# The start of the expert lookup on one core: the order of the first gate and norm steps, the placing of the query steps, and the batch sizes

## The chip, the cores and the metric

One core of a Trainium2 chip runs the kernel. Its five engines (TensorE or PE, VectorE or DVE, ScalarE or ACT, GpSimd or POOL, SyncE or SP) each run an instruction stream of their own and are ordered by semaphores alone. The metric is the device time of one execution in microseconds (us); several executions are run and their median is given.

## The reference, cut to what matters

The program computes two transformer blocks for 512 tokens of 1024 features. The last part of the second block, which the change touches, is a lookup of experts: each token picks, for each of 8 heads, the best 16 of 16384 one-neuron experts, and each pick needs that expert's row of `u_tab` and its row of `v_tab`.

```python
q = (xc @ w_pq).reshape(P_CHUNK, P_HEADS, 2, P_DK // 2)
s = jnp.einsum('thpd,hpkd->thpk', q, sub_keys)
s_top, i_top = lax.top_k(s, P_TOPK)                       # 16 of 128, two halves of each head
cand = s_top[..., 0, :, None] + s_top[..., 1, None, :]    # 16 x 16 candidates
best, ci = lax.top_k(cand.reshape(P_CHUNK, P_HEADS, P_TOPK * P_TOPK), P_TOPK)
e1 = jnp.take_along_axis(i_top[..., 0, :], ci // P_TOPK, axis=-1)
e2 = jnp.take_along_axis(i_top[..., 1, :], ci % P_TOPK, axis=-1)
expert = e1 * N_KEYS + e2
gate = jax.nn.softmax(best.astype(jnp.float32), axis=-1).astype(xc.dtype)
act = jax.nn.gelu(jnp.einsum('thkd,td->thk', u_tab[expert], xc), approximate=False)
return jnp.einsum('thk,thkd->td', gate * act, v_tab[expert])
```

`xc` is a normed and modulated copy of the stream x after attention, and the result is added to x before the last norm.

## The kernel before, in words

The 512 tokens are four tiles of 128. All stages up to attention (mixer, gated MLP, convolution, attention) run over all tiles; they are not touched. After them `first_tiles` works on tiles 0 and 1 (`k.late[0]`): output projections (`merge`, `out2_piece`), the second norm (`norm4`), its transposition (`transposed2`: PE turns the tile, DVE and ACT each copy half of it out), and the first four query columns of each tile (`first_queries(i, r)`, eight accumulating matmuls of 128x128 and a copy by ACT for each).

From then on each engine runs its `peer` loop. The picks of a tile are cut into batches of heads, listed in `k.order` (line 2668) as (tile, first head, heads). For tile 0 they are 1, 2, 2 and 3 heads, for each further tile 4 and 4. A head has 16 picks, and a pick is one indirect transfer by POOL (line 2569): 128 rows of 8 KB from the table of experts, u and v side by side, into one of 7 buffers (8 from pick 80, 12 from pick 208). The picks are worked on two at a time, a *group* (`groups`):

- DVE multiplies both rows with the token and adds up (line 2481), ACT takes the gelu (1732), DVE multiplies with the gate (2487), ACT writes two diagonal matrices (1737), PE multiplies them with the v halves into PSUM (1222). When PE has done a pick its buffer is free, and POOL may start the next gather into it (`s.picked`).
- POOL takes the gathers in order. Each batch begins with a wait on `s.expert`, which DVE raises when the batch's expert numbers are written (2420). The fifth gather of all goes to slot 0, a half of weight buffer 2. It waits on the last reader of that buffer, which is `first_queries(1, 3)` on PE.

Beside the groups run two further lists of steps. *Beside steps* (`k.beside`) are the lookup of the next batch, `route(b + 1)`: PE multiplies queries and keys, ACT copies the scores, DVE finds the top 16 in 17 steps; `steps(b)` of them are taken after each group: 3 in batches of one head, 2 of two heads, 1 of more. *Late steps* are the dense work for later: `queries2(0, ...)`, the remaining twelve query columns of tiles 0 and 1 (24 steps of eight matmul instructions; r = 4 to 15), and then `dense(1)`, the same chain for tiles 2 and 3. On PE one late step follows each group. ACT and DVE follow two steps behind (`lagging`). Before the peer loop `first_tiles` takes the first 8 steps of `queries2` at once (`for _ in range(8): next(rest)`), since the scores of the second batch need r = 2 to 5. Weights for the late steps come by SP in units of 2 MB into buffers 0 and 1 as these come free.

In `first_tiles` the orders of the engines around the change are these.

- DVE: `add_out2(1, 1)`, `norm4(1)`, then all of `route(0)`, with `transposed2(1)` after its sixth step.
- ACT: first queries of tile 0, scores of batch 0, `stack(0)` (three copies that lay tile 0 out for two picks at once), `transposed2(1)`, the four copies of `first_queries(1, r)`, the exponential of the first gates (rest of `routing`, line 1684), `stack(1)`, eight query steps.
- PE: scores of batch 0, `transposed2(1)`, `first_queries(1, 0..3)`, eight query steps, and then the groups.

Of the kernel before, what the change touches and what calls it, by code (L numbers as in the profile page):

```python
# [20 lines left out]
NT = SEQ // P  # L21
# [141 lines left out]
class Kernel:  # L163
# [53 lines left out]

    def steps(self, b):
        return 3 if self.picks(b) == TOPK else 2 if self.picks(b) < 3 * TOPK else 1

    def parts(self, b):

# [195 lines left out]
def tensor_program(k):  # L418
# [732 lines left out]
    def first_tiles():  # L1151
# [36 lines left out]
        pe.wait_ge(*ps.of["h2T", 1].free)  # L1188
        for r in range(4):
            first_queries(1, r)  # L1190
        rest = queries2(0, tiles_, 1)
        for _ in range(8):
            next(rest)
        return rest

    def route(b):
        i, h0, nh = k.order[b]
# [9 lines left out]
    def peer(rest):  # L1207
        late = chained(rest, dense(1))
        pick = 0
        for b, (i, h0, nh) in enumerate(k.order):  # L1210
# [4 lines left out]
            for g, (j0, size) in enumerate(k.groups(b)):  # L1215
                for half in range(2):
                    for x in range(size):
                        slot, loads, before = k.gathers[pick + x]
                        if half == 0:
                            pe.wait_ge(s.diag, pick + x + 1)  # L1220
                            pe.wait_ge(s.ld_slot[slot], 16 * loads)
                        last = pe.matmul(acc.pair[k.pick_rows(j0 + x), half, :], k.diags[(pick + x) % DIAGS],  # L1222
                                         k.slots[slot][:, D + half * 512:D + (half + 1) * 512],
                                         start=h0 == 0 and j0 + x < 2, stop=last_batch and j0 + x >= nh * TOPK - 2)
                        if half:
                            last.then_inc(s.picked)
                        elif pick + x == len(k.gathers) - 1:
                            last.then_inc(s.half_picked)
                pick += size
                if g == k.route_begins(b) and b + 1 < len(k.order):  # L1230
                    route(b + 1)
                next(late, None)
            if last_batch:
                ps.held.discard(acc.at)

# [13 lines left out]
def scalar_program(k):  # L1249
# [353 lines left out]
    def transposed2(i):  # L1603
        turn(("h2T", i), k.merged[:, :, i * P:(i + 1) * P], [k.ones[:, 0:1]] * KC)
# [33 lines left out]
    def first_tiles():  # L1638
# [21 lines left out]
        first_queries(0, 3)  # L1660
        stack(0)
        transposed2(1)
        for r in range(4):
            first_queries(1, r)
        for _ in routing:
            pass
        stack(1)
        rest = queries2(0, 4)
        for _ in range(8):
            next(rest)  # L1670
        return rest

    def route(b):
        i, h0, nh = k.order[b]
# [46 lines left out]

    def peer(rest):
        act.wait_ge(s.ident2, 1)
        late = k.lagging(chained(rest, dense(1)))
        pick = group = 0
        for b, (i, h0, nh) in enumerate(k.order):
            beside = k.beside(b, finish_tile, route)
            cf, hid = k.coef[b % 2], k.hidden[b % 2]
            for j0, size in k.groups(b):
# [8 lines left out]
                    pick += 1  # L1738
                for _ in range(k.steps(b)):
                    next(beside, None)  # L1740
                next(late, None)
            for _ in beside:
                pass
        finish_last()
# [14 lines left out]
def vector_program(k):  # L1759
# [558 lines left out]
    def first_tiles():  # L2318
# [14 lines left out]
        add_out2(0, 1)  # L2333
        transposed2(0)
        add_out2(1, 1)
        norm4(1)
        dve.wait_ge(*of["row", 3].free)
        for n, _ in enumerate(route(0)):
            if n == 5:
                transposed2(1)  # L2340
        return k.gap(2 * (2 * PH - 4 - 4))

    def transposed2(i):
        turn(("h2T", i), k.merged[:, :, i * P:(i + 1) * P], [k.ones[:, 0:1]] * KC)
# [26 lines left out]
    def route(b):  # L2371
# [46 lines left out]
        for a, src in enumerate((slice(0, PAIR), slice(PAIR, P))):  # L2418
            for c, dst in enumerate((slice(0, PAIR), slice(PAIR, P))):
                ins = dve.scalar_tensor_tensor(stacked[0][dst, :, :, a], first[src, :, :, c], float(NKEY), second[src, :, :, c], ALU.mult, ALU.add)  # L2420
        ins.then_inc(s.expert)
        dve.wait_ge(s.gate_exp, b + 1)
        dve.tensor_reduce(k.gsum[:, 0, 0:nh], g, AX_X, ALU.add).then_inc(v.up())
        dve.wait_ge(*v.now())
# [40 lines left out]
    def peer(rest):  # L2465
        late = k.lagging(chained(rest, dense(1)))
        pick = group = 0
        for b, (i, h0, nh) in enumerate(k.order):
# [5 lines left out]
            for j0, size in k.groups(b):  # L2474
# [12 lines left out]
                dve.tensor_tensor(cf[:, cut], cf[:, cut], g[:, cut], ALU.mult).then_inc(s.coef)  # L2487
                for _ in range(k.steps(b)):
                    next(beside, None)
                next(late, None)  # L2490
            for _ in beside:
                pass
        finish_last()
# [146 lines left out]
def program(nc, A, out):  # L2640
    with ExitStack() as stack:
# [15 lines left out]
        k.heads_order = [(h + a, i) for h in range(0, AH, 2) for i in range(NT) for a in range(2)]  # L2657
        k.feature_sq = [k.sg[1], k.sg[2], k.sg[1], k.sg[0]]
        k.feature_root = [k.sg[0], k.sg[2], k.sg[1]]
        k.order = [(0, 0, 1), (0, 1, 2), (0, 3, 2), (0, 5, 3)] + [(i, h0, 4) for i in range(1, NT) for h0 in (0, 4)]  # L2660
        count = [0] * 12
        k.gathers = []
        busy, free = {}, deque((2, 3, 4, 5, 0, 1, 6))
# [148 lines left out]
```

## Time and profile before

| | us |
|---|---|
| median of 3 runs | 2815.76 |
| lowest, highest | 2812.87, 2822.55 |
| the profiled execution | 2814.78 |
| its span in the trace | 2813.5 |

| engine | busy us | share of the span |
|---|---|---|
| PE (matmul) | 2291.8 | 81% |
| DVE | 1732.4 | 62% |
| POOL | 741.9 | 26% |
| ACT | 638.4 | 23% |

The span is the time from the first to the last instruction in the trace; 1.3 us of the profiled execution lie around it. The shares are averages over two different halves: to about 1430 us PE is busy nearly always, and from about 1450 us the DMA engines are. In the chain of work that ended last PE has 36% of the span and DMA 31%. All rows below come from the one profiled execution.

### The profile page before, as it was taken

The page shows a single profiled execution, that of the slowest core. Times are in us where ns is not written, and L with a number is a line of the kernel's source. Part 1 is how long each engine was busy: PE and PEld are TensorE (multiplying, and loading weights), DVE is VectorE, ACT ScalarE, POOL GpSimd, SP SyncE. Part 2 cuts the span into 40 slices and gives each one's busy share as a digit, 9 for nine tenths or more (in the row PEclk, how much of TensorE's full clock was granted, in tenths as well). Part 3 has the DMA queues.
Part 4 walks back from the last instruction along what each step waited for, and adds up shares of the span by engine and source line. Part 5 has one row for each costly group of instructions (what it writes and reads, how often), then busy time and mean ns, then how long its engine had stood idle before and what let it go on. Part 6 is the DMA issues. An engine that isn't in the chain of part 4 may idle for free.

```text
span 2813.5 us, 24680 instructions
## 1 busy us (share of the span) xinstructions
PE 2291.8 (81%) x8398; PEld 1294.5 (46%) x8398; DVE 1732.4 (62%) x3796; ACT 638.4 (23%) x1611; POOL 741.9 (26%) x582
## 2 busy tenths in 40 slices
PE   8998999999999999999997777678555656566655
PEld 5756478886444445666664433344222222222222
DVE  2132369985127995666447677767675767667555
ACT  2222220001020003566232111322112211121112
POOL 0000032430000002000014444434444444444442
PEclk9999999999999999999999999899888778787778
DMA  4111124443222121001359999999999999999997
GB/s 164 60 46 45 53 90 179 151 170 147 87 98 85 63 82 68 1 1 60 119 212 371 421 415 421 407 421 419 420 420 420 420 420 419 420 420 420 420 420 297
DMA packets 87307, 687.13 MB, mean 244 GB/s; under 512 B 9848, under 2 KB 10616, under 8 KB 12816
## 3 DMA queue, kind: packets, MB, share of 16 engines
q0 software_dynamic: 73728, 536.90, 46.2%
q1 hardware_dynamic: 12016, 144.09, 13.3%
q10 hardware_dynamic: 1440, 4.57, 0.4%
q8 instruction: 69, 1.13, 0.2%
q14 instruction: 54, 0.44, 0.0%
HBM read 683.42 MB, written 2.10 MB: 244 GB/s over the span
## 4 chain that ended last, share of the span: by engine, by line
PE 36%; DMA 31%; DVE 7%; ACT 3%; POOL 2%; issue 1%; ACTq 0%; DVEq 0%
PE psum L430 20%; DMA slot<-in_experts,expert 19%; DMA weights<-in_experts,expert 11%; PE psum L1222 5%; PE psum L1024 3%; DVE slot L2481 2%; PE psum L1046 2%; PE psum L1032 1%; DVE weights L2481 1%; PE psum L1095 1%; PE psum L1085 1%; POOL xn L2569 1%; PE psum L1117 1%; ACT spare_row L1737 1%; POOL weights L2569 1%
## 5 line engine op out<-in xcount | busy, mean ns | idle before, releaser
L1222 PE MATMUL psum<-slot,spare_row 128*64 128x512 f32 x844 | 387.2, 751 | 112.5 <-ACT spare_row L1737 112.5
L1222 PE MATMUL psum<-weights,spare_row 128*64 128x512 f32 x832 | 305.6, 782 | 190.6 <-ACT spare_row L1737 187.0
L2569 POOL DMA_INDIRECT slot<-in_experts,expert x211 | 251.4, 1192 | 544.4 <-DVE expert L2420 314.1
L1222 PE MATMUL psum<-xn,spare_row 128*64 128x512 f32 x372 | 223.7, 733 | 160.0 <-ACT spare_row L1737 159.0
L2569 POOL DMA_INDIRECT weights<-in_experts,expert x208 | 241.8, 1162 | 279.5 <-PE psum L1222 245.0
L1732 ACT ACTIVATE coef<-hidden 128x2 f32<-128x2 f32 (+1 forms) x257 | 52.3, 203 | 1003.4 <-DVE hidden L2481 1003.4
L1222 PEld LDWEIGHTS psum<-weights,spare_row 128*64 128x64 f32 x832 | 114.4, 164 | 358.5 <-ACT spare_row L1737 295.2
L2481 DVE CUSTOM_DVE_ANT_0 slot<-slot,h_late 128x1024 f32<-128x1024 f32 x147 | 180.0, 1225 | 126.2 <-DMA slot<-in_experts,expert 124.9
L430 PE MATMUL psum<-xnT,weights 128*128 128x264 f32 (+1 forms) x1040 | 245.2, 390 | 1.5 <-ACT mixedT L1399 0.9
L430 PE MATMUL psum<-hT,weights 128*128 128x512 f32 x560 | 243.0, 596 | 1.9 <-ACT hT L1266 1.9
L430 PEld LDWEIGHTS psum<-xnT,weights 128*128 128x128 f32 x1040 | 199.4, 194 | 37.7 <-issue 5.1
L1222 PEld LDWEIGHTS psum<-slot,spare_row 128*64 128x64 f32 x844 | 112.4, 159 | 213.1 <-ACT spare_row L1737 157.9
L2481 DVE CUSTOM_DVE_ANT_0 weights<-weights,h_late 128x1024 f32<-128x1024 f32 x104 | 127.5, 1226 | 96.5 <-DMA weights<-in_experts,expert 95.9
L2119 DVE SCALAR_TENSOR_TENSOR merged<-padded,cols,merged 128x512 f32<-128x512 f32 x240 | 175.2, 749 | 6.4
L1222 PEld LDWEIGHTS psum<-xn,spare_row 128*64 128x64 f32 x372 | 49.9, 156 | 275.4 <-ACT spare_row L1737 242.5
L430 PEld LDWEIGHTS psum<-hT,weights 128*128 128x128 f32 x560 | 106.7, 191 | 137.0 <-issue 134.9
L2523 POOL TENSOR_TENSOR up_sums<-weights 128x1024 f32<-128x1024 f32 x11 | 27.5, 2502 | 522.9 <-DMA weights<-in_w_up 489.8
L1737 ACT ACTIVATE spare_row<-ident,coef 128x64 f32<-128x64 f32 x512 | 150.3, 340 | 59.5 <-DVE coef L2487 59.5
L2569 POOL DMA_INDIRECT xn<-in_experts,expert x93 | 104.1, 1120 | 217.5 <-PE psum L1222 214.6
L2481 DVE CUSTOM_DVE_ANT_0 weights<-weights,hT 128x1024 f32<-128x1024 f32 x104 | 126.9, 1220 | 42.8 <-DMA weights<-in_experts,expert 42.4
L430 PE MATMUL psum<-weights,gT 128*128 128x512 f32 x352 | 152.1, 593 | 0.0
L2481 DVE CUSTOM_DVE_ANT_0 xn<-xn,hT 128x1024 f32<-128x1024 f32 x88 | 107.5, 1221 | 44.0 <-DMA xn<-in_experts,expert 43.8
(401 smaller groups left out, 3489.0 us busy)
## 6 DMA issues: line engine op xcount, KB each, us to landing
weights<-in_w_mod SPq DMA_DIRECT2D x12, 2048.0 KB, 8.5
weights<-in_w_up SPq DMA_DIRECT2D x11, 2048.0 KB, 7.5
weights<-in_w_in SPq DMA_DIRECT2D x8, 2048.0 KB, 8.4
weights<-in_w_pq SPq DMA_DIRECT2D x8, 2048.0 KB, 10.3
weights<-in_w_out SPq DMA_DIRECT2D x6, 2048.0 KB, 9.2
weights<-in_w_in_t SPq DMA_DIRECT2D x4, 2048.0 KB, 7.7
weights<-in_w_down SPq DMA_DIRECT2D x4, 2048.0 KB, 12.4
weights<-in_w_o_mla SPq DMA_DIRECT2D x4, 2048.0 KB, 10.0
```

The costliest lines, as they stand in the source:

```text
L430: last = pe.matmul(out, lhsT, rhs, start=start and n == 0, stop=stop and n == len(pairs) - 1)
L1024: last = pe.matmul(u.pair[:, a, 0:KH], Q[0:QK, h % 4, i * P:(i + 1) * P], K[0:QK, h % 2, a * KH:(a + 1) * KH], start=True, stop=True)
L1032: last = pe.transpose(u.pair[:, j // 3, (j % 3) * P:(j % 3 + 1) * P], L[:, j * P:(j + 1) * P], ident[:])
L1046: last = pe.matmul(u.pair[rows, 0, 0:2 * P], k.values[j][:, (2 * p + a) * VD:(2 * p + a + 1) * VD], k.probsT[q][:, j, a * 2 * P:(a + 1) * ...
L1085: last = pe.matmul(u.pair[:, 0, 0:len(tiles_) * P], w[:, c, v * P:(v + 1) * P], k.heads[:, cut, c, :], start=c == 0, stop=c == KC - 1)
L1095: last = pe.matmul(u.pair[:, 0, :], k.merged[:, c, i * P:(i + 1) * P], w[:, c, :], start=c == 0, stop=c == KC - 1)
L1222: last = pe.matmul(acc.pair[k.pick_rows(j0 + x), half, :], k.diags[(pick + x) % DIAGS], k.slots[slot][:, D + half * 512:D + (half + 1) * 512],
L1732: act.activation(cf[:, j0:j0 + size], hid[:, j0:j0 + size], ACT.Gelu).then_inc(s.gelu)
L1737: act.activation(k.diags[pick % DIAGS], k.ident2[:], ACT.Copy, scale=cf[:, j:j + 1]).then_inc(s.diag)
L2119: ins = dve.scalar_tensor_tensor(acc, src, col(k, "dw_w", j * KC + n), acc, ALU.mult, ALU.add)
L2481: ins = dve.tensor_tensor_reduce(slot[:, 0:D], slot[:, 0:D], rows_of[j % 2], 1.0, 0.0, ALU.mult, ALU.add, hid[:, j:j + 1])
L2569: pool.indirect_dma_start(k.slots[slot], None, k.A["experts"], bass.IndirectOffsetOnAxis(ap=k.expert[b % 2][:, j:j + 1], axis=0))\
```

## The change

It does five things. On DVE `norm4(1)` moves behind the first 18 steps of `route(0)`, that is, behind the expert numbers of the first batch (a new `yield` after `then_inc(s.expert)` makes the place), and `transposed2(1)` moves behind the end of `route(0)`. On ACT the exponential of the first gates moves ahead of the copies of `first_queries(1, r)`, and `stack(1)` moves behind the query steps (`later_tiles`). The eight query steps ahead of the peer loop go on every engine. In the first two batches two late steps follow each group instead of one (`late_steps`). The batches of tile 0 are 1, 1, 2 and 4 heads instead of 1, 2, 2 and 3.

```diff
--- before.py
+++ after.py
@@ -218,6 +218,9 @@
     def steps(self, b):
         return 3 if self.picks(b) == TOPK else 2 if self.picks(b) < 3 * TOPK else 1
 
+    def late_steps(self, b):
+        return 2 if b < 2 else 1
+
     def parts(self, b):
 
         h0, nh = self.order[b][1:]
@@ -1188,10 +1191,7 @@
         pe.wait_ge(*ps.of["h2T", 1].free)
         for r in range(4):
             first_queries(1, r)
-        rest = queries2(0, tiles_, 1)
-        for _ in range(8):
-            next(rest)
-        return rest
+        return queries2(0, tiles_, 1)
 
     def route(b):
         i, h0, nh = k.order[b]
@@ -1229,7 +1229,8 @@
                 pick += size
                 if g == k.route_begins(b) and b + 1 < len(k.order):
                     route(b + 1)
-                next(late, None)
+                for _ in range(k.late_steps(b)):
+                    next(late, None)
             if last_batch:
                 ps.held.discard(acc.at)
 
@@ -1660,15 +1661,16 @@
         first_queries(0, 3)
         stack(0)
         transposed2(1)
+        for _ in routing:
+            pass
         for r in range(4):
             first_queries(1, r)
-        for _ in routing:
-            pass
+        return queries2(0, 4)
+
+    def later_tiles(rest):
+        yield from rest
         stack(1)
-        rest = queries2(0, 4)
-        for _ in range(8):
-            next(rest)
-        return rest
+        yield from dense(1)
 
     def route(b):
         i, h0, nh = k.order[b]
@@ -1721,7 +1723,7 @@
 
     def peer(rest):
         act.wait_ge(s.ident2, 1)
-        late = k.lagging(chained(rest, dense(1)))
+        late = k.lagging(later_tiles(rest))
         pick = group = 0
         for b, (i, h0, nh) in enumerate(k.order):
             beside = k.beside(b, finish_tile, route)
@@ -1738,7 +1740,8 @@
                     pick += 1
                 for _ in range(k.steps(b)):
                     next(beside, None)
-                next(late, None)
+                for _ in range(k.late_steps(b)):
+                    next(late, None)
             for _ in beside:
                 pass
         finish_last()
@@ -2333,12 +2336,15 @@
         add_out2(0, 1)
         transposed2(0)
         add_out2(1, 1)
+        routing = route(0)
+        for _ in range(18):
+            next(routing)
         norm4(1)
+        for _ in routing:
+            pass
         dve.wait_ge(*of["row", 3].free)
-        for n, _ in enumerate(route(0)):
-            if n == 5:
-                transposed2(1)
-        return k.gap(2 * (2 * PH - 4 - 4))
+        transposed2(1)
+        return k.gap(2 * (2 * PH - 4))
 
     def transposed2(i):
         turn(("h2T", i), k.merged[:, :, i * P:(i + 1) * P], [k.ones[:, 0:1]] * KC)
@@ -2419,6 +2425,7 @@
             for c, dst in enumerate((slice(0, PAIR), slice(PAIR, P))):
                 ins = dve.scalar_tensor_tensor(stacked[0][dst, :, :, a], first[src, :, :, c], float(NKEY), second[src, :, :, c], ALU.mult, ALU.add)
         ins.then_inc(s.expert)
+        yield
         dve.wait_ge(s.gate_exp, b + 1)
         dve.tensor_reduce(k.gsum[:, 0, 0:nh], g, AX_X, ALU.add).then_inc(v.up())
         dve.wait_ge(*v.now())
@@ -2487,7 +2494,8 @@
                 dve.tensor_tensor(cf[:, cut], cf[:, cut], g[:, cut], ALU.mult).then_inc(s.coef)
                 for _ in range(k.steps(b)):
                     next(beside, None)
-                next(late, None)
+                for _ in range(k.late_steps(b)):
+                    next(late, None)
             for _ in beside:
                 pass
         finish_last()
@@ -2657,7 +2665,7 @@
         k.heads_order = [(h + a, i) for h in range(0, AH, 2) for i in range(NT) for a in range(2)]
         k.feature_sq = [k.sg[1], k.sg[2], k.sg[1], k.sg[0]]
         k.feature_root = [k.sg[0], k.sg[2], k.sg[1]]
-        k.order = [(0, 0, 1), (0, 1, 2), (0, 3, 2), (0, 5, 3)] + [(i, h0, 4) for i in range(1, NT) for h0 in (0, 4)]
+        k.order = [(0, 0, 1), (0, 1, 1), (0, 2, 2), (0, 4, 4)] + [(i, h0, 4) for i in range(1, NT) for h0 in (0, 4)]
         count = [0] * 12
         k.gathers = []
         busy, free = {}, deque((2, 3, 4, 5, 0, 1, 6))
```

## Rows read from the trace of the kernel before

**Rows 1.** Page, span in 40 equal slices: GB/s that the DMA engines moved.

```profile
GB/s 164 60 46 45 53 90 179 151 170 147 87 98 85 63 82 68 1 1 60 119 212 371 421 415 421 407 421 419 420 420 420 420 420 419 420 420 420 420 420 297
```

**Rows 2.** Page, DMA queue: packets, MB, share.

```profile
q0 software_dynamic: 73728, 536.90, 46.2%
```

**Rows 3.** Windows: PE, PEld, DVE, ACT, POOL busy; PEclk, DMA share, GB/s.

```profile
1442.00:1448.00 6.00, 4.99 (x23) 5.00 (x24) 4.29 (x18) 1.23 (x5) 1.04 (x1) 0.50 0.00 0
1448.00:1452.00 4.00, 4.00 (x38) 4.00 (x37) 0.00 (x0) 0.55 (x2) 2.91 (x4) 1.00 0.84 274
1472.00:1482.00 10.00, 9.53 (x43) 5.80 (x43) 8.36 (x38) 1.53 (x5) 4.32 (x6) 1.00 0.97 346
1482.00:1494.00 12.00, 8.82 (x35) 4.94 (x34) 11.07 (x31) 2.05 (x8) 5.52 (x4) 1.00 1.01 418
1494.00:1504.70 10.70, 8.19 (x32) 4.74 (x32) 9.92 (x28) 4.44 (x9) 1.51 (x2) 1.00 0.42 158
1448.00:1516.00 68.00, 53.96 (x252) 36.90 (x250) 40.84 (x123) 19.63 (x47) 24.95 (x23) 1.00 0.88 346
1600.00:1650.00 50.00, 38.63 (x151) 21.87 (x148) 39.21 (x128) 9.63 (x29) 19.84 (x17) 0.93 1.01 418
```

**Rows 4.** Timeline, first lookup: start, us, engine, line, operation.

```profile
1433.23 0.16 DVE L1765 RECIPROCAL stat<-stat 128x1 f32<-128x1 f32 x1 [1.54 <-ACT stat L1259]
1434.69 0.39 ACT L1273 ACTIVATE scores<-psum 128x256 f32<-128x256 f32 x1 [0.58 <-PE psum L1204]
1435.89 0.48 DVE L2348 MAX8 top<-scores 128x8 f32<-128x128 f32 x2
1438.70 1.13 DVE L1777 TENSOR_SCALAR merged<-psum,ones 128x128 f32<-128x128 f32 x4
1439.75 0.42 DVE L2386 TENSOR_TENSOR scores<-top 128x256 f32<-128x256 f32 x1
1445.98 0.69 DVE L2420 SCALAR_TENSOR_TENSOR expert<-picked 64x8 uint32<-64x8 f32 x4
```

**Rows 5.** Timeline, POOL: first, fifth, eighth and seventeenth gather.

```profile
1446.96 1.12 POOL L2569 DMA_INDIRECT slot<-in_experts,expert  x1 [304.68 <-DVE expert L2420]
...
1453.05 0.94 POOL L2569 DMA_INDIRECT weights<-in_experts,expert  x1 [1.23 <-PE psum L430]
...
1471.60 0.94 POOL L2569 DMA_INDIRECT slot<-in_experts,expert  x1 [15.12 <-PE psum L1222]
...
1502.88 0.94 POOL L2569 DMA_INDIRECT slot<-in_experts,expert  x1 [9.47 <-DVE expert L2420]
```

**Rows 6.** Timeline, second tile's transposes, query matmuls, and the first gates.

```profile
1438.07 1.04 PE L441 MATMUL psum<-ident,hT 128*128 128x128 f32 x8
...
1441.81 1.14 ACT L1266 ACTIVATE merged<-psum,ones 128x128 f32<-128x128 f32 x4
...
1443.01 9.77 PE L430 MATMUL psum<-merged,weights 128*128 128x128 f32 x64 [3.90 <-ACT merged L1266]
...
1454.40 0.22 ACT L1684 ACTIVATE gate_exp<-gate_exp 128x16 f32<-128x16 f32 x1
...
1454.65 0.17 DVE L2423 TENSOR_REDUCE gsum<-gate_exp 128x1 f32<-128x16 f32 x1 [7.97 <-ACT gate_exp L1684]
...
1455.05 0.69 DVE L2430 TENSOR_TENSOR gate<-gate_exp,gsum 64x8 f32<-64x8 f32 x4
```

**Rows 7.** Timeline, the block ahead of the first group, and the first groups.

```profile
1452.61 13.98 PE L1117 MATMUL psum<-merged,weights 128*128 128x256 f32 x64
...
1467.03 1.28 ACT L1732 ACT_TABLE_LOAD   x1
...
1469.43 2.03 PE L1222 MATMUL psum<-slot,spare_row 128*64 128x512 f32 x8 [2.84 <-ACT spare_row L1737]
...
1472.38 1.89 PE L1117 MATMUL psum<-merged,weights 128*128 128x256 f32 x8
1474.20 1.94 PE L1222 MATMUL psum<-slot,spare_row 128*64 128x512 f32 x8
```


## The prediction

> **What bounds the kernel now.** I read the page's slices first. To about 1430 us the DMA engines are far from full; from 1548 us on they move 407 to 421 GB/s in every slice but the last [rows 1]. The software queue alone carries 536.90 MB [rows 2], which is 512 gathers of 1.049 MB (128 rows of 8 KB). So the second half of the span is a stream of gathers at about 420 GB/s, 2.5 us each, and engine work beside it costs nothing unless it starves the stream. The span can change in two ways only: the stream starts earlier or later, or it has fewer or more holes. That is read from the windows at its start, then from the timelines of the engines that feed it.
>
> Between 1442 and 1448 nothing moves [rows 3]. The first gather is issued at 1446.96 [rows 5], and between 1448 and 1452 the DMA share is 0.84 [rows 3]: moving begins 0.16 x 4 = 0.64 us after 1448, some 1.7 us after the issue. From 1448 to 1516 the mean is 346 GB/s, 23.5 MB [rows 3]. At 420 it would be 28.6 MB; the missing 5.0 MB are 12.0 us. About half of that is one hole: between 1494 and 1504.7 the share is 0.42 [rows 3], 6.2 us idle, because the seventeenth gather (first of the second batch) waited for its expert numbers until 1502.88, with POOL idle for 9.47 us [rows 5]. The rest is a low rate: 346 GB/s from 1472 to 1482, against 418 from 1482 to 1494 [rows 3]. The tail after the last gather is untouched. So 12.0 us of holes and a later or earlier start are all that is at stake, 0.4% of the time.
>
> **The change part by part.**
>
> *Norm behind the first expert numbers.* DVE's lookup began at 1435.89, behind the norm, though its scores were there at 1434.69 + 0.39 = 1435.08: 0.8 us. `transposed2(1)` inside the lookup took from 1438.70 to 1439.75: 1.05 us [rows 4]. Without both, the numbers that were done at 1445.98 + 0.69 = 1446.67 are done at 1444.8, and the first gather is issued at 1445.1 rather than 1446.96, 1.85 us earlier. Taken alone this is the gain that the edit aims at.
>
> *What the norm delays.* The norm took from 1433.23 to the end of its last operation just after 1435.89, 2.75 us with the overlap [rows 4]; it now ends at 1447.6. Then a chain follows that lay under other work before:
> - PE's eight transposes, 1.04 us at the full clock [rows 6], up to twice that at half: PE's work before them ends as the transposes of before begin, about 1438.1, so it has been idle for over 9 us. I take 1449.2.
> - ACT's `transposed2(1)`, 1.14 us [rows 6]: 1450.4.
> - the exponential: a table load of 1.28 [rows 7] and 0.22 [rows 6]: 1451.9. (Before, it was done at 1454.62.)
> - DVE's gates, which are ahead of its `transposed2(1)` in the new order: from 1454.65 to 1455.74, 1.1 us [rows 6]: 1453.0. Behind this wait on DVE are queued `transposed2(1)` and the first products.
> - DVE's `transposed2(1)`, 1.13 us [rows 4]: 1454.2.
> - PE's `first_queries(1, 0..3)`, 64 instructions: 9.77 us [rows 6], half of it at the low clock: the granted clock was 0.50 from 1442 to 1448 [rows 3]. They begin at 1454.3 rather than 1443.01 and end at 1464.1 rather than 1452.78.
>
> The last line is the important one. The fifth gather waits for exactly this end: it was issued at 1453.05, and POOL had sat idle 1.23 us for PE's query matmuls [rows 5]. POOL is in order, so the sixth and seventh are queued behind it. After the change the fifth goes out at 1464.1 + 0.27 = 1464.4. Four gathers, 4.19 MB, move from 1446.8 and at 346 to 420 GB/s are done between 1456.8 and 1458.9; then the DMA engines have nothing (SP's next weights wait on PE too) until 1464.4 + 1.7 = 1466.1. So the hole at 1494 is exchanged for one of 7 to 9 us at 1458, and the 1.85 us are worth nothing, since the same four gathers are done before 1464 either way.
>
> *The query block taken out.* The block of 64 instructions held PE from 1452.61 for 13.98 us [rows 7]. Without it PE and ACT reach the first group straight after the queries: last copy at about 1464.4, and from there as before from 1467.03 (table load) to 1469.43 (first matmul), 2.4 us [rows 7]: the first group at 1466.8 instead of 1469.43, the eighth gather at 1469.0 instead of 1471.60 [rows 5].
>
> *Two steps after each group.* PE's group becomes 1.94 us of picks and two steps of 1.82 to 1.89 [rows 7], 5.6 us. DMA needs 2 x 2.5 = 5.0 us a group, and eight steps, which are four groups, release a weight unit of 2 MB, 5.0 us more: 25.0 us of DMA work for 22.4 us of PE. In the mean DMA stays the slower one. ACT takes a query copy a group behind PE, so it waits for a step that ended before PE began the group.
>
> *Batches 1, 1, 2, 4.* The second batch's lookup has one head, like the first's, 1446.67 - 1435.89 - 1.05 = 9.7 us of DVE [rows 4], spread over groups 1 to 6 (three steps each). Group 5's matmuls begin at 1466.8 + 0.6 + 5 x 5.6 = 1495.4 (0.6 for the scores' matmuls, an estimate from a step's 1.89 for eight instructions). From there ACT's copy 0.4, table 1.3, gelu and gate 0.4 lead to group 6's gate at 1497.5, and the last sixth of the lookup, 1.6, to the numbers at 1499.1: the seventeenth gather at 1499.4, moving at 1501.1, against 1502.88 before. By then DMA has had, from 1466.1, twelve gathers and the fourth query unit (now released by step 8, about 1490): 12 x 2.5 + 5.0 = 35.0 us, to 1501.1. The hole just closes. The third batch's two heads are looked up beside one head's groups, as the second batch's were before, but with another weight unit in the queue. The fourth batch's four heads are looked up at two steps a group where three were: the nearest rows are the window 1600 to 1650, DVE busy 39.2 of 50 us with the DMA share at 1.01 [rows 3]. One head more adds a third to three heads' lookup; by 9.7 us a head that is at most 9.7 on about 52 us for nine groups, so DVE's 41 become 51. It just fits. I take 0, with 0 and 5 us as ends.
>
> *`stack(1)` later.* Three copies, off the path before; they now meet the second batch's exponential in one group of ACT. 0, at most 1 us.
>
> *Sum.* By 1516 the kernel before has moved 23.5 MB. After, 4.19 MB by 1466, and then 49.9 us at a rate that I take between its two neighbours, 346 for 10 us and 418 for 12 [rows 3], 385 GB/s: 19.2 MB, 23.4 in all. 0.1 MB short is 0.3 us at 420. At 418 throughout it is 25.0 MB, 3.7 us gained; at 346, 21.5 MB, 4.9 lost. Query matmuls without a low clock would be 2.3 us shorter. The profiled execution took 2814.8, 1.0 below the median of the runs; with 0.3 more it is 2815.1. I say 2815.
>
> **The rivals.**
> 1. *The restart isn't held.* If the fifth gather went out at its old place behind the fourth, the hole at 1458 is not there, and of 12.0 us only the ramp is left, about 1: 2804. For it: this is what the edits would give with the fifth buffer free. Against it: the row of the fifth gather names PE's query matmuls as what released it, and nothing in the diff frees that buffer sooner. The same number would come if the norm's chain were much shorter than I work out.
> 2. *PE stays cold: slower.* PE is idle twice, from 1438.1 to 1447.6 and from 1449 to 1454, where there was one gap of 3.9 us, after which the clock was 0.50, the 1.2 GHz level, for 6 us [rows 3, 6]. If it stays there through the queries and the first group, the 64 instructions take about 15 us instead of 9.77 (+5.1), and the first group 11.2 instead of 5.6 (+5.6): 10.7 us more hole, 2825. It decides from the second group at the low clock on. Against it: in the trace the clock was back at 1.00 in the window from 1448, 5 us after work began, and PE then has work without a break. The Trainium skill, TensorE: Matmul & The Clock Gate, Part 1, says that the throttled state is the default and that only sustained activity releases it. By that rule the two gaps speak against this change; the trace agrees on the fall and on the return.
> 3. *PE becomes the feed's limit.* If weight units don't fill the gaps, 16 groups lose 0.6 us each, 9.6 us, less up to 5 us that a unit hides: 2820 to 2825. For it: 5.6 is more than 5.0. Against it: seven buffers hold 17.5 us of transfers.
>
> **How the numbers follow.** A difference of 0.3%, 8.4 us, is about what a measurement of this kernel can tell. Forecast 0.68 (2815, its own range 2809 to 2822, within 0.3%). Rival 1 0.10 (faster). Rival 2 0.13 (slower). Rival 3 0.09, two thirds of it within 0.3% of the median of before. So faster 0.10, same 0.74, slower 0.16. The range 2807 to 2825 leaves out rival 1 and the upper part of rival 2.
>
> **What would show it.** Right: first gather 1.9 us earlier, fifth some 11 us later behind PE's L430, an empty DMA window from 1458 to 1466, no POOL wait for expert numbers of more than a few us before the seventeenth, DMA at 1.0 from 1505 on. Wrong: a fifth gather before 1460; clock 0.50 beyond 1461; DMA shares below 0.95 between 1510 and 1640, which would put the loss into the two steps a group or the four heads.

## The result, and the profile after

| | before | after |
|---|---|---|
| median of 20 runs each | 2818.47 us | 2827.15 us |
| lowest, highest | 2808.37, 2829.31 | 2816.97, 2837.17 |
| ratio after / before, 95% interval | | 1.0024 (1.0013 to 1.0036) |
| the profiled execution, its span | 2814.78, 2813.5 | 2825.49, 2824.2 |

The change costs 0.24%, 6.8 us. That is within the 0.3% that the forecast gave as the likeliest, but the time lies 2 us above the stated range. The two spans are 10.7 us apart, and not all of that is the change: the copy of the first scores, ahead of which nothing is altered, comes at 1437.95 after and came at 1434.69 before [rows 4]. From that copy to the end it is 1386.2 us against 1378.8: 7.4 us in these two executions, close to the 6.8 of the medians' ratio.

To see where they went I count *lost transfer time*: from 5 us after the first scores' copy to 1300 us after it, the span is cut into stretches, and each stretch loses its length times (420 - GB/s) / 420, by the windows. If transfers are what limits this part, the difference of the sums must be near the 7.4 us, and it is: 30.2 - 23.2 = 7.0.

| us after the first scores' copy | before | after |
|---|---|---|
| 5 to 22, start of the stream | 10.4 | 7.9 |
| 22 to 32 | -0.1 | 9.1 |
| 32 to 60 | 2.8 | 3.0 |
| 60 to 81, ahead of the second batch | 7.3 | 0.1 |
| *up to 81* | *20.4* | *20.1* |
| 100 to 140, ahead of the third batch | 0.0 | 3.7 |
| 140 to 240, beside the fourth batch's lookup | 0.7 | 5.0 |
| 240 to 450 | 2.0 | 1.5 |
| sum | 23.2 | 30.2 |

The windows behind it, of the kernel after (first two: 4 us each, from 12 and from 20 us after the copy; then 22 to 32, 60 to 81, 100 to 140, 140 to 240), in the columns of [rows 3]:

```profile
1450.00:1454.00 4.00, 1.97 (x8) 1.57 (x8) 0.97 (x1) 0.96 (x4) 3.39 (x3) 0.50 0.91 328
1458.00:1462.00 4.00, 3.96 (x18) 3.96 (x19) 2.28 (x4) 0.14 (x1) 0.00 (x0) 0.50 0.71 299
1459.95:1469.95 10.00, 8.20 (x57) 8.01 (x56) 0.33 (x2) 2.57 (x6) 1.22 (x2) 0.81 0.09 36
1497.95:1518.95 21.00, 20.09 (x89) 13.05 (x89) 11.43 (x29) 5.08 (x14) 7.59 (x8) 1.00 1.00 417
1537.95:1577.95 40.00, 35.17 (x157) 23.14 (x157) 28.45 (x74) 12.17 (x29) 12.54 (x12) 1.00 0.94 381
1577.95:1677.95 100.00, 74.08 (x249) 33.72 (x245) 78.78 (x224) 17.84 (x58) 41.88 (x34) 0.93 0.98 399
```

The same three last stretches of the kernel before:

```profile
1494.69:1515.69 21.00, 14.07 (x56) 7.96 (x56) 14.80 (x34) 5.82 (x15) 8.98 (x7) 1.00 0.69 273
1534.69:1574.69 40.00, 28.73 (x114) 16.46 (x112) 29.46 (x77) 9.13 (x27) 16.39 (x14) 0.95 1.01 420
1574.69:1674.69 100.00, 76.47 (x276) 39.85 (x272) 73.57 (x200) 17.23 (x58) 42.41 (x35) 0.92 1.01 417
```

The hole ahead of the second batch (273 GB/s before) is closed (417), but between 22 and 32 us almost nothing moves (36 GB/s, share 0.09); and the two later stretches, full before at 420 and 417, run at 381 and 399.

The timeline of the kernel after, from the first scores to the eighth gather, which answers to [rows 4 to 7]:

```profile
1437.95 0.38 ACT L1274 ACTIVATE scores<-psum 128x256 f32<-128x256 f32 x1 [0.58 <-PE psum L1204]
1438.37 0.49 DVE L2354 MAX8 top<-scores 128x8 f32<-128x128 f32 x2 [3.42 <-ACT scores L1274]
...
1447.48 0.69 DVE L2426 SCALAR_TENSOR_TENSOR expert<-picked 64x8 uint32<-64x8 f32 x4
1448.46 1.12 POOL L2577 DMA_INDIRECT slot<-in_experts,expert  x1 [302.91 <-DVE expert L2426]
...
1449.75 1.23 DVE L2292 TENSOR_TENSOR hT<-hT,ctxn 128x1024 f32<-128x1024 f32 x1
1451.03 1.97 PE L444 MATMUL psum<-ident,hT 128*128 128x128 f32 x8 [9.54 <-DVE hT L2292]
...
1453.04 1.15 ACT L1267 ACTIVATE merged<-psum,ones 128x128 f32<-128x128 f32 x4 [7.99 <-PE psum L444]
...
1455.49 0.22 ACT L1686 ACTIVATE gate_exp<-gate_exp 128x16 f32<-128x16 f32 x1
...
1456.14 0.69 DVE L2437 TENSOR_TENSOR gate<-gate_exp,gsum 64x8 f32<-64x8 f32 x4
1456.87 1.12 DVE L1780 TENSOR_SCALAR merged<-psum,ones 128x128 f32<-128x128 f32 x4
1458.05 10.11 PE L433 MATMUL psum<-merged,weights 128*128 128x128 f32 x64 [5.05 <-DVE merged L1780]
...
1468.42 0.94 POOL L2577 DMA_INDIRECT weights<-in_experts,expert  x1 [14.16 <-PE psum L433]
...
1470.88 3.50 PE L1222 MATMUL psum<-slot,spare_row 128*64 128x512 f32 x8 [2.73 <-ACT spare_row L1739]
1474.59 0.94 POOL L2577 DMA_INDIRECT slot<-in_experts,expert  x1 [2.39 <-PE psum L1222]
```

After the lookup come first gather, norm, transposes, ACT's half, exponential, gates, DVE's half, queries, fifth gather and first group, in the order that the prediction works out. The brackets name the step ahead as what ended the wait at the transposes (norm), ACT's half (transposes), the queries (DVE's half) and the fifth gather (queries). The fifth gather is issued 30.5 us after the scores' copy; before it was 18.4 us [rows 4, 5].

Two waits of POOL for expert numbers remain, and the second one is what the third batch costs (columns as in the timelines above; POOL, DVE, ACT, DVE, POOL):

```profile
1504.92 0.93 POOL L2577 DMA_INDIRECT slot<-in_experts,expert  x1 [6.83 <-DVE expert L2426]
...
1554.53 1.22 DVE L2488 CUSTOM_DVE_ANT_0 slot<-slot,h_late 128x1024 f32<-128x1024 f32 x1 [1.65 <-DMA slot<-in_experts,expert]
...
1555.80 0.20 ACT L1734 ACTIVATE coef<-hidden 128x2 f32<-128x2 f32 x1 [1.06 <-DVE hidden L2488]
...
1558.28 0.72 DVE L2426 SCALAR_TENSOR_TENSOR expert<-picked 64x16 uint32<-64x16 f32 x4
...
1559.26 0.93 POOL L2577 DMA_INDIRECT weights<-in_experts,expert  x1 [12.01 <-DVE expert L2426]
```

The first (6.83 us) costs nothing, since the queue still holds gathers. In the second POOL sits idle 12.01 us. The last products of the group ahead of the numbers themselves waited for a gather (1.65 us, at 1554.53); gelu, gate and the last lookup steps follow, and the numbers are there at 1559.0. By then the stream has run dry:

```profile
1558.00:1560.00 2.00, 2.00 (x10) 1.15 (x7) 1.86 (x8) 0.00 (x0) 0.74 (x1) 1.00 0.20 82
```

Beside the fourth batch's lookup DVE is the slow one. In this window of the kernel after (columns of [rows 3]) it is busy 21.68 of 23 us while the stream falls to 337 GB/s:

```profile
1603.00:1626.00 23.00, 16.11 (x66) 8.89 (x64) 21.68 (x61) 5.98 (x15) 10.12 (x8) 0.99 0.91 337
```

The first products of one group and of the fourth group after it, in the timeline, are 25.5 us apart: 6.4 us a group, where a group's two gathers take 5.0.

```profile
1602.44 1.21 DVE L2488 CUSTOM_DVE_ANT_0 slot<-slot,hT 128x1024 f32<-128x1024 f32 x1
...
1627.98 1.22 DVE L2488 CUSTOM_DVE_ANT_0 slot<-slot,hT 128x1024 f32<-128x1024 f32 x1
```

### The profile page after: what moved, and what is told of

Same layout as the page of the kernel before. It is cut to its first block, busy times and chain, and to the rows that moved or that the text cites. A ratio compares the mean times of both kernels' runs of the same rounds, so it can differ in the third digit from the quotient of the medians.

```text
span 2824.2 us, 24682 instructions
## 1 busy us (share of the span) xinstructions
PE 2299.0 (81%) x8398; PEld 1294.6 (46%) x8398; DVE 1731.4 (61%) x3796; ACT 639.0 (23%) x1611; POOL 739.3 (26%) x582
## 4 chain that ended last, share of the span: by engine, by line
PE 34%; DMA 31%; DVE 7%; ACT 3%; POOL 2%; issue 2%; ACTq 0%; DVEq 0%; POOLq 0%
PE psum L433 19%; DMA slot<-in_experts,expert 16%; DMA weights<-in_experts,expert 15%; PE psum L1222 5%; PE psum L1027 3%; DVE slot L2488 2%; PE psum L1049 2%; PE psum L1035 1%; DVE weights L2488 1%; PE psum L1098 1%; PE psum L1088 1%; POOL weights L2577 1%; PE psum L1120 1%; ACT spare_row L1739 1%; POOL slot L2577 1%
## 5 line engine op out<-in xcount | busy, mean ns | idle before, releaser
L1222 PE MATMUL psum<-slot,spare_row 128*64 128x512 f32 x844 | 397.1, 762 | 100.3 <-ACT spare_row L1739 100.3
L1222 PE MATMUL psum<-xn,spare_row 128*64 128x512 f32 x372 | 239.5, 779 | 165.2 <-ACT spare_row L1739 163.5
## 6 DMA issues: line engine op xcount, KB each, us to landing
weights<-in_w_down SPq DMA_DIRECT2D x4, 2048.0 KB, 12.2
```

## Experiments

All ten kernels, beside the two. "Span" is the time from the first scores' copy to the end, less that of before; the sum is that of the lost transfer time, less 23.2.

| kernel | 5 to 22 | 22 to 32 | 32 to 60 | 60 to 81 | 100 to 140 | 140 to 240 | sum | span | ratio to before (95%) |
|---|---|---|---|---|---|---|---|---|---|
| after | 7.9 | 9.1 | 3.0 | 0.1 | 3.7 | 5.0 | +7.0 | +7.4 | 1.0024 (1.0013 to 1.0036) |
| norm_only | 7.9 | 9.1 | 8.5 | 5.5 | 0.1 | -0.2 | +13.1 | +13.4 | 1.0046 (1.0023 to 1.007) |
| norm_back | 9.8 | -0.1 | 4.0 | 1.4 | 2.4 | 4.5 | -0.7 | -0.7 | 0.9998 (0.9981 to 1.0015) |
| slot6_fifth | 7.8 | 6.7 | 5.3 | 0.1 | 4.6 | 4.3 | +7.5 | +7.7 | 1.0029 (1.0009 to 1.0049) |
| heads_1133 | 8.0 | 9.0 | 2.7 | 0.6 | 7.2 | 0.0 | +4.2 | +5.7 | 1.0024 (0.9998 to 1.005) |
| stack_back | 8.1 | 8.5 | 5.9 | 1.4 | 1.9 | 5.5 | +8.5 | +9.0 | one run |
| unit_off | 8.0 | 8.6 | 0.5 | 0.3 | 7.7 | 5.0 | +8.6 | +3.8 | one run |
| steps4 | 7.9 | 9.1 | 2.5 | -0.1 | 0.0 | 5.2 | +2.3 | +1.9 | 1.0000 (0.9978 to 1.0022) |
| spread | 8.0 | 9.0 | 2.3 | 0.0 | -0.2 | 1.4 | -1.2 | -1.6 | 0.9977 (0.9964 to 0.9989) |
| four_ahead | 9.8 | -0.1 | 1.1 | 1.9 | 0.0 | 0.0 | -7.9 | -7.5 | 0.9975 (0.9955 to 0.9995) |
| four_ahead_s4 | 10.3 | -0.2 | 1.6 | -0.1 | 0.0 | 0.0 | -7.5 | -8.4 | 0.9983 (0.9964 to 1.0001) |

81 to 100 (norm_only 3.5, all others within 0.1) and 240 to 450 us (0.0 to 4.0) are in the sums. Each kernel's stretches come from one profiled execution. Sum and span agree within 1 us but for two kernels: unit_off moves 2 MB (4.8 us) less, and in heads_1133 1.5 us stay unexplained.

### The norm's part: norm_only and norm_back

To the kernel before, on DVE (and on ACT the rest of `routing` ahead of `first_queries(1, r)`):

```diff
-        norm4(1)
-        dve.wait_ge(*of["row", 3].free)
-        for n, _ in enumerate(route(0)):
-            if n == 5:
-                transposed2(1)
+        routing = route(0)
+        for _ in range(18):
+            next(routing)
+        norm4(1)
+        for _ in routing:
+            pass
+        dve.wait_ge(*of["row", 3].free)
+        transposed2(1)
```

> The kernel before with only the first part of the change: norm, second tile's transposes and the first gates' exponential in the new order; the block of eight query steps, one step a group and batches 1, 2, 2, 3 as before. Theory: the fifth gather goes out about 30 us after the first scores' copy, with the same empty stretch of some 9 us; the block of 14 us then holds the first group until about 46 us after the scores, 11 us later than before, so that a second empty stretch of some 6 us follows when the seven gathers are done; in all 10 to 14 us over before, 0.4 to 0.5%. Rival (the early expert numbers pay for the wait): 2 us under to 3 us over before.

Two of its windows, 22 to 32 and 32 to 60 us after its scores' copy at 1443.89:

```profile
1465.89:1475.89 10.00, 10.00 (x67) 9.77 (x67) 0.32 (x2) 2.65 (x6) 1.32 (x2) 0.82 0.09 39
1475.89:1503.89 28.00, 24.69 (x108) 17.13 (x107) 10.37 (x44) 7.42 (x17) 5.89 (x7) 0.94 0.79 292
```

Share 0.09, then 292 GB/s, and 13.4 us in the span: the theory's 10 to 14. So the edit that was to bring the first gather forward costs 13 us by itself, with the query block still ahead of the groups. norm_back takes the same edit out of the kernel after:

> The changed kernel with the order of the norm, the second tile's transposes and the first gates' exponential put back as before; query steps between the groups and batches 1, 1, 2, 4 stay. I count lost transfer time from the copy of the first scores on: (420 - GB/s) / 420 times the length of each window. The changed kernel lost 30.5 us in all, 18.0 of it by 81 us after that copy, where the kernel before lost 23.3 and 20.5. Theory (the hole comes from the fifth gather waiting for the second tile's queries, which the norm's chain delays): fifth gather about 18 us after the scores' copy instead of 30, no empty stretch from 22 to 32 us, the first group some 10 us earlier than in either kernel; lost by 81 us about 12, so 6 us less than the changed kernel, and a time about that of before or just under it. The later losses (3.8 us at the third batch, 4.9 us at the fourth batch's lookup) stay. Rival (two query steps a group limit the feed, and the hole only delays what PE could not take anyway): lost by 81 us stays at 17 to 18 and the time at that of the changed kernel, 0.24% over before.

The 18.0 us that this expectation gives for the kernel after up to 81 us are 20.1 in the table, so its "6 us less" is 14 by the table, and the rival's unchanged value is 20. Its fifth gather and its first group (scores' copy at 1439.63):

```profile
1458.10 0.94 POOL L2574 DMA_INDIRECT weights<-in_experts,expert  x1 [1.36 <-PE psum L433]
...
1465.68 3.77 PE L1222 MATMUL psum<-slot,spare_row 128*64 128x512 f32 x8 [7.85 <-ACT spare_row L1739]
```

The fifth gather is out 18.5 us after the scores' copy, the hole is gone, the first group comes at 26.1 us instead of 32.9, and lost time up to 81 us falls from 20.1 to 15.1, 5.0 less (the first group was expected some 10 us earlier and came 7 earlier, and it took 3.77 us for 2.03 [rows 7]). The time can't be told from that of before. The theory holds, and the rival, by which that loss would not change, falls.

### Which of the two waits behind the norm: slot6_fifth

```diff
-        busy, free = {}, deque((2, 3, 4, 5, 0, 1, 6))
+        busy, free = {}, deque((2, 3, 4, 5, 6, 0, 1))
```

> The changed kernel with one edit: the buffers are given out in the order 2, 3, 4, 5, 6, 0, 1 instead of 2, 3, 4, 5, 0, 1, 6, so the fifth gather goes to a buffer that is free, and the sixth is the first that waits for the second tile's queries. Theory (the stretch of 9.1 us without transfers is the wait on that buffer): five gathers move before the restart, the empty stretch falls by one gather, 2.5 us, to 6.6, and the time by 0 to 2.5 us. Rival (the restart is set by the first group, not by the buffer): the fifth gather goes out early, but the bytes moved by 81 us after the first scores are the same within 0.3 MB.

22 to 32 and 32 to 60 us after its scores' copy at 1444.51:

```profile
1466.51:1476.51 10.00, 8.15 (x57) 7.96 (x56) 0.32 (x2) 2.60 (x6) 1.28 (x2) 0.82 0.33 138
1476.51:1504.51 28.00, 27.12 (x114) 16.42 (x115) 19.91 (x60) 7.62 (x24) 11.13 (x10) 0.94 0.94 341
```

The first window gains 2.4 us (138 GB/s), the second loses 2.3 (341): up to 81 us 19.9 against 20.1, less than 0.1 MB apart. The rival is right here. The buffer makes the visible wait, but the same chain holds the first group as well, and a gather brought forward without a group brought forward moves nothing.

### The later losses: heads_1133, steps4 and spread

```diff
-k.order = [(0, 0, 1), (0, 1, 1), (0, 2, 2), (0, 4, 4)]
+k.order = [(0, 0, 1), (0, 1, 1), (0, 2, 3), (0, 5, 3)]
```

> The changed kernel with batches of 1, 1, 3, 3 heads instead of 1, 1, 2, 4. Theory (each later loss is a lookup that is too large for the groups that it lies beside): the loss at the fourth batch's lookup, 4.9 us at 165 to 200 us after the first scores, falls to under 1 us, as three heads at one step a group leave DVE time; the hole at the third batch's expert numbers grows from 3.8 us to 6 to 8, since three heads are looked up beside eight groups. In all within 2 us of the changed kernel. Rival (both losses come from the two late steps a group and the weights that they call up earlier): both stay where they are, 3.8 and 4.9 us.

100 to 140 and 140 to 240 us after its scores' copy at 1444.04:

```profile
1544.04:1584.04 40.00, 33.53 (x145) 22.27 (x144) 32.71 (x83) 11.25 (x26) 11.74 (x12) 1.00 0.85 344
1584.04:1684.04 100.00, 74.39 (x243) 34.49 (x241) 71.11 (x191) 17.78 (x59) 39.60 (x37) 0.91 1.01 420
```

3.7 becomes 7.2, and 5.0 becomes 0.0, as the theory has it: each loss goes with the size of one lookup. steps4 instead takes the kernel after and gives the lookups beside one-head batches four steps a group instead of three:

```diff
-        return 3 if self.picks(b) == TOPK else 2 if self.picks(b) < 3 * TOPK else 1
+        return 4 if self.picks(b) == TOPK else 2 if self.picks(b) < 3 * TOPK else 1
```

> The changed kernel with four lookup steps instead of three after each group of the batches of one head. The third batch's expert numbers then come one group earlier in the second batch. Theory (the hole at the third batch is the place of the numbers behind the seventh group): loss from 100 to 140 us from 3.8 to under 1.5; the 4.9 us at the fourth batch stay; 2 to 4 us under the changed kernel. Rival (DVE is the limit there, and more steps a group make each group longer by as much): 3 to 5 us lost as before, or earlier in the batch.

The same two stretches of it, scores' copy at 1428.80:

```profile
1528.80:1568.80 40.00, 38.39 (x172) 24.11 (x170) 29.95 (x78) 12.32 (x28) 15.94 (x14) 1.00 1.01 420
1568.80:1668.80 100.00, 76.44 (x243) 33.91 (x244) 78.35 (x232) 18.00 (x59) 42.63 (x35) 0.88 0.99 398
```

420 GB/s: with the numbers one group earlier the hole at the third batch is gone, and the 5.2 us beside the fourth batch's lookup are left. The span is 5.5 us under the kernel after, more than the expected 2 to 4. spread adds to steps4 a slower lookup beside the third batch, two steps and one in turn (after group n, where the call in the loop over groups becomes `steps_after`):

```diff
+    def steps_after(self, b, n):
+        return 2 - n % 2 if b == 2 else self.steps(b)
...
-            for _ in range(k.steps(b)):
+            for _ in range(k.steps_after(b, n)):
```

> The changed kernel with four lookup steps a group in the batches of one head (which lost 25.4 us, 5.2 of it from 140 to 240 us after the first scores), and in the third batch two and one steps in turn instead of two after each group, so that the fourth batch's four heads are looked up over 12 groups instead of 9. Theory (DVE is the limit in those nine groups): the loss from 140 to 240 us falls from 5.2 to under 2, 22 to 23 us lost in all. Rival (the loss there comes from the low clock of PE or from the order of the steps, not from DVE's work per group): it stays at 4 to 6, or the numbers come too late for the 65th gather and open a new hole of 3 us or more at its end.

140 to 240 us after its scores' copy at 1440.76:

```profile
1580.76:1680.76 100.00, 76.87 (x248) 34.99 (x248) 81.31 (x242) 18.01 (x59) 45.24 (x36) 0.93 1.01 414
```

5.2 falls to 1.4 with DVE busier than before (81.3 of 100 us against 78.4). So it was not DVE's work as such, but that nine groups had to carry it. The time is under that of before by 6.5 us over seven runs (3 to 10), the span of the profiled execution by only 1.6; how much of the 6.5 is a first half that came early by chance stays open.

### One execution each: stack_back and unit_off

> The changed kernel with ACT's stack(1), three copies of 1.05 us, back ahead of the groups. In the changed kernel it lies in the same group of the second batch as the exponential and two table loads, 6 us of ACT in a row that end 1.1 us before the next gelu. Theory (the hole at the third batch, 3.8 us, comes from the lookup being queued on DVE behind the products of the seventh group, not from ACT): the hole stays at 3 to 5 us. Rival (the moved copies delay the gelu and so the expert numbers): it falls by 2 to 3 us.

```diff
             first_queries(1, r)
+        stack(1)
         return queries2(0, 4)
```

(and its call in `later_tiles` taken out.) Its stretch from 100 to 140 us:

```profile
1540.42:1580.42 40.00, 38.67 (x171) 24.81 (x168) 31.93 (x84) 9.28 (x27) 15.14 (x14) 0.97 0.98 400
```

The loss there fell to 1.9, between the two expectations; but the copies now hold the first group, 35.1 us after the scores' copy instead of 32.9, and 32 to 81 us lost 4.2 more. A start that differs changes what the queue holds at the third batch, so the run doesn't separate the two.

> The changed kernel with one weight unit not loaded (64 KB of 2 MB of the second w_o_mla unit of tiles 2 and 3, so that their output is worked out from what lay in the buffer): the one that SP issues 106 us after the first scores, beside the last gathers of the second batch. Prediction's view (the unit fills the queue while the third batch's numbers are worked out): without it the loss from 100 to 140 us grows from 3.8 to about 8 us, and the span loses nothing. Rival (the unit delays the gathers that the lookup itself waits for, so it hides nothing): the loss stays at about 4 us, the numbers come some 4 us earlier, and the span falls by the unit's 5 us.

```diff
-                weights(name, unit)
+                weights(name, unit, P if (tiles_, name, unit) == (k.late[1], "w_o_mla", 1) else UNIT)
```

100 to 140 us after its scores' copy at 1442.07:

```profile
1542.07:1582.07 40.00, 37.14 (x168) 23.64 (x164) 29.31 (x78) 12.05 (x27) 14.04 (x14) 1.00 0.84 339
```

7.7 us lost instead of 3.7, 4.0 more, what the prediction's view has. The gather that waits for the numbers also went out 3.3 us earlier (118.0 us after the scores' copy against 121.3), and the span is 3.6 us shorter where 4.8 us of transfers are gone. But not all of that is the edit's: up to 81 us, ahead of the unit, this execution had already lost 2.6 us less (17.5 against 20.1), with the same program. Its first group took 2.03 us where that of the kernel after took 3.50, behind an idle time of the same length:

```profile
1474.06 2.03 PE L1222 MATMUL psum<-slot,spare_row 128*64 128x512 f32 x8 [2.73 <-ACT spare_row L1739]
```

At the last gather of the second batch (107.17 us after the copy against 108.24) 1.1 us of that lead were left, so about 2.2 of the 3.3 us can be the unit's, and of the 3.6 us in the span about 1.0. The unit mainly fills the queue; that it also delays the gathers that the lookup waits for is likely, by some 2 us, but one execution with another start doesn't show it alone.

### Four query steps ahead of the groups: four_ahead and four_ahead_s4

To the kernel before, in the norm's old order and with batches 1, 2, 2, 3, and with two of the late query steps a group in the first batch and one in the others (the loops of PE and of ACT; left out here are `late_steps`, which gives 2 for the first batch and 1 for the others, and DVE's count of the steps that it skips):

```diff
-        for _ in range(8):
+        for _ in range(4):
             next(rest)
...
-                next(late, None)
+                for _ in range(k.late_steps(b)):
+                    next(late, None)
```

> The kernel before with one edit: four query steps instead of eight ahead of the groups (the second batch's scores need no more) and two steps a group in the first batch; order of the norm and batches 1, 2, 2, 3 as before. Theory (the first group, not the first gather, sets what the stream loses in its first 81 us): first group about 27 us after the first scores instead of 35, the hole of 7.3 us ahead of the second batch falls to 1 to 3, in all 17 to 19 us lost instead of 23.3, 0.15 to 0.2% under before. Rival (two steps a group slow the first batch by what the earlier start gains): 22 to 24 us lost, time as before.

60 to 81 us after its scores' copy at 1448.11:

```profile
1508.11:1529.11 21.00, 16.85 (x66) 9.97 (x65) 10.82 (x27) 2.54 (x10) 7.96 (x8) 0.92 0.94 381
```

7.3 us become 1.9, 15.3 are lost in all (expected: 17 to 19), and the time is 0.25% under before (0.05 to 0.45). Half of the query block was not needed before the second batch's scores, and it had held the first group, which comes 26.9 us after the scores' copy instead of 34.7. With four lookup steps a group beside the first batch (the steps4 edit on this kernel):

> The kernel with four query steps ahead (order of the norm and batches 1, 2, 2, 3 as before the change), and four lookup steps instead of three after each group of the first batch. It lost 15.3 us with three, of which 1.9 between 60 and 81 us after the first scores, ahead of the second batch's numbers. Theory (numbers one group earlier close that hole): 1.9 falls to under 0.6, the rest stays, 13 to 15 us lost in all, 0.2 to 0.35% under before. Rival (DVE is full in the first batch, so four steps make each group longer): 15 to 17 us lost, time as with three steps.

```profile
1502.32:1523.32 21.00, 18.31 (x84) 12.14 (x84) 9.59 (x19) 3.31 (x12) 8.43 (x8) 1.00 1.01 421
```

The last hole is closed (421 GB/s from 60 to 81 us), as the theory has it, but 15.7 us are lost in all, in the rival's range, since 240 to 450 us lost 4.0 instead of 2.5 in these executions. The time can't be told from that of four_ahead, nor, by its interval, from that of before.

## Why the prediction was wrong

**The first 81 us: right.** The sum was 0.3 us worse than before; the lost time is 0.3 better, 20.1 against 20.4. The steps hold one by one, measured from the scores' copy: first gather at 10.5 us against 12.3 before, 1.8 earlier (worked out: 1.85); fifth at 30.5 against 18.4, 12 later (11 to 12); an empty stretch of 9.1 us (7 to 9); the seventeenth gather waits for its numbers without a hole (worked out: just closes). POOL's 6.83 us ahead of it are more than the "few us" among the signs, and cost nothing. That the two sums meet within 0.6 us is in part luck: unit_off, the same program up to there, lost 2.6 us less. Rival 1 is out: the fifth gather waited 14.16 us for PE's query matmuls. Its price was too high as well, since norm_back, which has no such wait, still loses 15.1 us up to 81 us.

**The cold clock: a small part of rival 2.** The granted clock was 0.50, the 1.2 GHz level, at 1450 to 1454 and at 1458 to 1462, after PE had been idle 9.54 and then 5.05 us. During the queries it rose to 1.00, and behind the 2.73 us without work ahead of the first group it fell again:

```profile
1464.00:1466.00 2.00, 2.00 (x21) 2.00 (x20) 0.00 (x0) 0.28 (x1) 0.00 (x0) 1.00 0.00 0
...
1472.00:1474.00 2.00, 2.00 (x7) 0.47 (x3) 0.70 (x3) 0.79 (x3) 0.19 (x1) 0.51 0.98 385
```

The queries took 10.11 us instead of 9.77, the first group 3.50 instead of 2.03: 1.8 us of the 10.7. Before the change the first group began at 1.00 behind 2.84 us without work, and in unit_off behind 2.73, so this gap alone doesn't settle the level. The Trainium skill, TensorE: Matmul & The Clock Gate, Part 1, says that activity releases the throttle. The trace agrees: the return to 1.00 came during the queries.

**The third batch: a step without a price.** The prediction said that its lookup runs as the second's did before, "with another weight unit in the queue", and put no number on it. It cost 3.7 us. The unit did fill the queue (without it 7.7 us are lost, unit_off), but the numbers come only behind the seventh of eight groups, whose own products waited for a gather (1.65 us). With the numbers one group earlier the loss is gone (steps4). The pattern was in the trace of before: the hole ahead of its second batch is the same place.

**The fourth batch's lookup: the wrong end.** "It just fits. I take 0, with 0 and 5 us as ends" was 5.0. The step added one head's 9.7 us to DVE's busy time and held the sum, 51 us, against the 52 us that nine groups took. But how long those groups took was set by the stream, which was itself the limit there (share 1.01 [rows 3]); what counts is DVE's time for a group against the 5.0 us of the group's two gathers. From 1603 to 1626 it was busy for 94% of the time and needed 6.4 us a group, and the stream fell to 337 GB/s. With 12 groups instead of 9 it is 1.4 (spread), with three heads 0.0 (heads_1133).

**The rest.** Rival 3 put such losses down to PE's two steps a group. The kernel spread keeps the two steps and has -0.2 and 1.4 in the two stretches, so it was not that. The prediction's own sign for these losses, DMA shares below 0.95 between 1510 and 1640, did come (0.94 and 0.91 in the windows above). Of the 12.2 us between 2815 and 2827.15, 2.7 are the median of before, which 20 runs put at 2818.47 instead of 2815.76, 1.0 is the profiled execution that the sum was made against, and 8.7 are the change by the two medians (6.8 by the ratio) against the 0.3 that I worked out. So the time is above the range by 2 us only because the median of before moved too: 8.7 on the old 2815.76 would have been inside it.

## What to carry to other kernels

Where a stream of transfers is the limit, count the bytes that it is behind, stretch by stretch, and price each edit by what it adds to that: a transfer brought forward gains nothing if the next one waits for a chain that the same edit makes longer. Price every place where a batch must wait for its numbers, also those that look like one already seen: numbers that stand behind the last groups of the batch ahead came too late ahead of the second batch of the kernel before and ahead of the third of the kernel after. And hold an engine's added work against the stream's time per group, not against a stretch that the stream itself had drawn out.

## What was not expected of the hardware

The untouched first half varies more than the change moves: in the twelve profiled executions the first scores' copy came between 1428.80 us (steps4) and 1448.11 us (four_ahead), though no edit changes the work ahead of it. The granted clock of PE differs between them; from 300 to 350 us, for one, it was 0.93 in steps4 and 0.86 in four_ahead. That the clock makes all of the difference is not shown. This spread is why the stretches here are counted from that copy, and why a change of 7 us was measured over 20 runs each.

The level of the clock differs between executions of the same instructions too: the first group took 3.50 us in the kernel after and 2.03 in unit_off, behind the same 2.73 us without work, and up to 81 us the two lost 20.1 and 17.5 us.
